# Expert 0's gate and up products ahead of the last two groups of the gather, in PSUM bank 6

## What is computed

```python
g_p, g_idx = lax.top_k(jax.nn.softmax(g_logits, axis=-1), 1)      # one of 4 groups
e_top, e_idx = lax.top_k(e_logits, TOP_K_IN_GROUP)                # 2 of its 8 experts
gate = g_p * jax.nn.softmax(e_top, axis=-1)
...
def expert_block(args):
    xb, e = args
    return (jax.nn.silu(xb @ w_gate[e]) * (xb @ w_up[e])) @ w_down[e]
...
x = x + hier_moe(h2, ...)
return rmsnorm_2(x, norm_f_g)
```

## Time and profile before

| | |
|---|---|
| runs of the kernel | 764.04, 763.16, 762.18 us; median 763.16 |
| profiled execution | span 760.7 us from the first to the last instruction (its time on the device is not listed apart; the median lies 2.5 us above the span) |
| TensorE busy | 727.5 us, 96% of the span |
| VectorE, ScalarE, GpSimd busy | 364.0, 324.0, 80.4 us |
| read from HBM | 179.91 MB |
| granted clock of TensorE, mean | 0.986 of 2.4 GHz |

### The profile page before, as it was taken

The page is one execution under the profiler, slowest core; times in us unless marked ns, Lnnn a source line. Parts: engine busy times, 40 slices in busy tenths (PEclk is TensorE's granted clock), DMA queues, the critical chain, the costliest instruction groups (busy, mean ns, idle before and its releaser), DMA issues.

```text
span 760.7 us, 11630 instructions
## 1 busy us (share of the span) xinstructions
PE 727.5 (96%) x4414; PEld 528.2 (69%) x4414; DVE 364.0 (48%) x602; ACT 324.0 (43%) x534; POOL 80.4 (11%) x58
## 2 busy tenths in 40 slices
PE   7999999899999999989999999988999999999994
PEld 6887864789999999959979999866333333333332
DVE  3244433656655655865544646655233323333224
ACT  3143444355445445554626443333334333343333
POOL 0000000132344332310030000000000000000001
PEclk9999999999999999999999999978999999999998
DMA  8951313245545545533423455482999999999992
GB/s 354 424 194 56 111 55 117 104 168 174 208 172 180 206 165 185 202 111 111 167 111 120 158 191 197 166 337 88 393 423 422 424 423 423 423 422 423 424 420 90
DMA packets 25237, 181.48 MB, mean 239 GB/s; under 512 B 2800, under 2 KB 3056, under 8 KB 3568
## 3 DMA queue, kind: packets, MB, share of 16 engines
q1 hardware_dynamic: 25056, 180.90, 60.7%
q10 hardware_dynamic: 144, 0.07, 0.0%
HBM read 179.91 MB, written 1.05 MB: 238 GB/s over the span
## 4 chain that ended last, share of the span: by engine, by line
PE 84%; DVE 6%; DMA 4%; ACT 2%; issue 1%; POOL 1%; SPq 0%; POOLq 0%; DVEq 0%; ACTq 0%
PE psum L861 39%; PE psum L1079 13%; PE psum L1092 6%; PE psum L1101 5%; PE psum L557 4%; PE psum L655 4%; DMA HN<-units_in 3%; PE psum L565 3%; PE psum L614 2%; DVE ffn_w_low L448 2%; PE psum L1071 1%; POOL rstd L1638 1%; DVE arena L1909 1%; PE psum L1050 1%; ACT ffn_w_high L443 1%
## 5 line engine op out<-in xcount | busy, mean ns | idle before, releaser
L448 DVE TENSOR_TENSOR ffn_w_low<-ring,ffn_w_high 128x2048 fp32r<-128x2048 f32 x57 | 134.7, 2364 | 119.5 <-ACT ffn_w_high L443 119.4
L443 ACT ACTIVATE ffn_w_high<-ring 128x2048 fp32r<-128x2048 f32 x57 | 109.3, 1918 | 144.9 <-PE psum L861 144.6
L861 PE MATMUL psum<-ht_high,ffn_w_high 128*128 128x256 f32 x576 | 163.8, 284 | 2.3 <-DVE ht_low L1893 1.3
L861 PE MATMUL psum<-ht_low,ffn_w_high 128*128 128x256 f32 x576 | 163.0, 283 | 0.0
L861 PE MATMUL psum<-ht_high,ffn_w_low 128*128 128x256 f32 x576 | 163.0, 283 | 0.0
L861 PEld LDWEIGHTS psum<-ht_high,ffn_w_high 128*128 128x128 f32 x576 | 110.4, 192 | 4.1 <-issue 2.1
L861 PEld LDWEIGHTS psum<-ht_low,ffn_w_high 128*128 128x128 f32 x576 | 110.5, 192 | 0.3
L861 PEld LDWEIGHTS psum<-ht_high,ffn_w_low 128*128 128x128 f32 x576 | 110.5, 192 | 0.0
L1254 ACT ACTIVATE arena<-psum 64x512 f32<-64x512 f32 (+6 forms) x96 | 43.0, 453 | 128.8 <-PE psum L1079 102.3
L2223 DVE TENSOR_TENSOR arena<-psum,arena 64x512 f32<-64x512 f32 x32 | 21.9, 684 | 126.4 <-ACT arena L1254 126.4
L1638 POOL TENSOR_TENSOR rstd<-ms,neghalf 128x1 f32<-128x1 f32 (+3 forms) x19 | 15.2, 803 | 509.1 <-DVE ms L1692 369.8
(11 more groups left out here) (308 smaller groups left out, 1104.0 us busy)
## 6 DMA issues: line engine op xcount, KB each, us to landing
ring<-units_in SPq DMA_DIRECT2D x117, 1024.0 KB, 5.0
more_units<-units_in SPq DMA_DIRECT2D x32, 1024.0 KB, 17.1
HN<-units_in SPq DMA_DIRECT2D x8, 1024.0 KB, 18.2
rows<-units_in SPq DMA_DIRECT2D x8, 1024.0 KB, 17.3
rows<-rows_in SPq DMA_DIRECT2D x1, 1688.0 KB, 12.6
arena<-bias_in SPq DMA_DIRECT2D x1, 1536.0 KB, 15.9
small<-small_in SPq DMA_DIRECT2D x1, 1232.0 KB, 25.4
const<-const_in SPq DMA_DIRECT2D x1, 1073.0 KB, 23.2
```

What stands on the lines that cost most here:

```text
L443: nc.scalar.activation(parts_slot(n)[0], w, ACT.Copy).then_inc(hi_ready, 1)
L448: nc.vector.tensor_tensor(l, ring[:, n % RING, :], h.bitcast(fp32), SUB).then_inc(lo_ready, 1)
L861: last = mm(o, l[a], r[b], start=start and (a, b) == pairs[0], stop=stop and (a, b) == pairs[-1])
```

## The change

The products of expert 0 move from behind the whole gather to behind its group 5, that is between groups 5 and 6 (the second half of the slots is groups 4 to 7). They are written into bank 6 instead of bank 0, and ScalarE and VectorE read them there. TensorE waits for `xw_ready` 1 at the new place; the wait for `xs_act` 4 falls away. SyncE's program and the order of the instructions on ScalarE and VectorE are as they were.

```diff
+        FIRST_AFTER, FIRST_BANK = 5, 6
...
+            def expert_up(x, w, ks, bank=0):
+
+                for k in ks:
+                    a, r = k % HALF_K * 2 * D_EXP, CH * (k % 2)
+                    last = mm(psum[r:r + CH, bank, :], x[:, k, :], w[:, a:a + 2 * D_EXP], start=k < 2, stop=k >= KD - 2)
+                return last
...
                 last.then_inc(xs_done, 1)
-
-            def expert_up(x, w, ks):
-
-                for k in ks:
-                    a, r = k % HALF_K * 2 * D_EXP, CH * (k % 2)
-                    last = mm(psum[r:r + CH, 0, :], x[:, k, :], w[:, a:a + 2 * D_EXP], start=k < 2, stop=k >= KD - 2)
-                return last
+                if g == FIRST_AFTER:
+                    pe.wait_ge(xw_ready, 1)
+                    for h in range(2):
+                        expert_up(XW[:, 0], unit(pe, U_EXP + h), range(h * HALF_K, (h + 1) * HALF_K), FIRST_BANK
+                                  ).then_inc(unit_used, 1)
...
-            pe.wait_ge(xs_act, 4)
-            pe.wait_ge(xw_ready, 1)
-            for g in range(2):
-                expert_up(XW[:, 0], unit(pe, U_EXP + g), range(g * HALF_K, (g + 1) * HALF_K)).then_inc(unit_used, 1)
             pe.wait_ge(table_in, 1)
...
-                copy(TS[0:CH, :], psum[CH:P, 0, :]).then_inc(low_half, 1)
+                copy(TS[0:CH, :], psum[CH:P, FIRST_BANK if e == 0 else 0, :]).then_inc(low_half, 1)
...
-                tt_op(UG[0:CH, :], psum[0:CH, 0, :], TS[0:CH, :], ADD).then_inc(up_summed, 1)
+                tt_op(UG[0:CH, :], psum[0:CH, FIRST_BANK if e == 0 else 0, :], TS[0:CH, :], ADD).then_inc(up_summed, 1)
```

## The result

| | median, us | runs | ratio to before, 95% interval |
|---|---|---|---|
| before | 762.75 | 5 | |
| after | 766.71 | 5 (765.22 to 768.23) | 1.0054 (1.0034 to 1.0073) |
| after, measured again beside the experiments | 766.28 | 8 (763.61 to 768.26) | 1.0058 (1.0037 to 1.0080) |

The change makes the kernel slower by 0.54 to 0.58%, 4.1 to 4.4 us; 2.3 us were forecast. The interval does not hold 1.0, so the loss is clear of the noise, small as it is. The plain difference of the medians is 3.96 us in both comparisons. The profiled execution of after has a span of 764.9 us against 760.7, and its own time is 766.71.

What follows compares the result with a forecast made beforehand. The prediction took the weight stream to set the end, with TensorE having slack. Its terms, +3.6 - 1.3 + 0 = +2.3 us on a median of 763.16, gave 765.5 us, range 763.7 to 767.2.

Steps and rivals of the forecast that it cites:

- The bound: End of the expert stage: the weight stream sets the end, and TensorE has 2.5 us of slack.
- Term 1: SyncE's issue into rows: released later because the gather's group 7 ends later, +3.6 us on the stream's start.
- Term 2: First 9 us of the weight stream: three queued units remove the 361 GB/s dip, -1.3 us, bounds 0 and -2.1.
- Term 3: TensorE from expert 1 on: 2.6 us later, covered by slack at the end, so 0 us.
- The cover: End of the kernel: TensorE's 2.5 us slack plus the stream's 2.3 us delay, 4.8 us, absorbs TensorE's 2.6 us lateness.
- Rival B: TensorE around expert 1: the clock falls after a thin stretch; 767.5 us if for 8 us of dense work; chance 0.07.
- Rival A: Start of the weight stream: nothing is caught up, 361 GB/s for its first 9 us; +3.6 us, 766.8 us; chance 0.15.
- Rival C: First 2.83 us of the weight stream: queued units fill the engines faster, catch-up -2.1 us, 764.7 us; chance 0.15.
- Rival D: TensorE sets the end and expert 0's sums overlap groups 6 and 7; -0.5 us, 762.7 us; chance 0.06.

Runs made afterwards that it cites:

- e1: The changed kernel with expert 0's products put back behind the whole gather, still in bank 6; 762.18 us, ratio 0.9994 to before.
- e5: The changed kernel with expert 0's copies, sums and SiLU ahead of the last gather takes, expert 1's window start loaded early; 764.89 us, ratio 1.0033 to before.
- e11: The changed kernel again, not edited, profiled once more; 765.94 us, a single run.
- e10: The changed kernel again, not edited, for one look at its profile; 766.09 us, a single run.
- e2: The kernel before with only SyncE's issue into rows held back until expert 0's second half unit is used; 764.54 us, ratio 1.0018 to before.
- e4: The changed kernel with useless matmuls in TensorE's idle time, one before the table and two behind it; 764.68 us, ratio 1.0024 to before.
- e7: The changed kernel again, not edited, beside other experiments; 766.28 us, eight runs.
- e12: The kernel before again, not edited, for one look at its profile; 759.09 us, a single run.
- e6: The changed kernel with the edits of e3 and e5 together; 762.87 us, ratio 1.0010 to before.
- e8: e6 with one useless matmul added between the gather and the table; 762.58 us, ratio 1.0008 to before.
- e3: The changed kernel with SyncE issuing the two units freed by expert 0's products ahead of the one into rows; 764.95 us, ratio 1.0036 to before.

## Why the prediction was right in its sign and too small

**The bound.** Right: the stream of weights sets the end in all profiles, and e1 shows that the place makes the loss.

**Term 1, +3.6 us on the stream's start.** Right in kind, a little small. With an ordinary gather the issue into rows stands 13.1 to 13.3 us behind the gather's start (e5, e11, e10) against 9.3: +3.8 to 4.0. Of this 3.58 are the products; groups 6 and 7 take 2.10 us behind them in place of 1.87. In the profile shown first, another 0.9 was the late rise of the clock in the gather, which is chance.

**Term 2, -1.3 us of catch-up.** This is the step that failed. The mechanism was right as long as TensorE is in time: e2, e4 and e5 have the full rate at once, and their streams are 1.1 to 2.2 us shorter than those of before. In the changed kernel next to nothing was caught up (213.1 to 213.9 against 213.2 to 214.2), because the fourth and fifth unit came late: 6.9 and 9.9 us behind the issue into rows, where e4 has them 6.1 and 8.3 us behind it, and the full rate. The prediction's test was too weak as well: it asked only that the fourth come before the work queued is done. The fourth did, at 540.70, 3.2 us before the third landed (543.9), and still the fourth, fifth and sixth landed 2.8, 3.2 and 3.6 us apart in place of 2.5. Why the DMA slows down while units are still under way is not shown.

**Term 3, 0 us for TensorE's lateness.** Its size without the clock was right: 2.6 us forecast for expert 1's start, and 537.76 - 534.25 = 3.5 measured, of which 0.9 is the later end of the gather. The cover was judged wrongly. The 4.8 us of slack at the end do cover TensorE's own work. But a late TensorE also releases slots late, and in its first 20 us the stream has none to spare. The prediction checked this only for the fourth unit and only with the fast clock.

**Rival B, the clock, at 0.07.** It took place in all four profiles. The mean clock of a run cannot tell whether it also did in the others: after has 0.982, and so have e4 and e5, without the fall. The clock fell after 4.03 us with 1.08 busy, and not after the stretch from 136.25 to 140.89, 4.64 us with 2.16 busy. Its price was sought at the end of the kernel, where the slack covers it, and not at the release of units. With e4 beside the changed kernel the fall costs 1.1 to 1.9 us of stream (212.0 against 213.1 to 213.9), and by the ratios, 1.0024 against 1.0054 and 1.0058, 2.3 to 2.6 us, of which the late rise in the gather may be a part. The Trainium skill ("TensorE: Matmul & The Clock Gate", section "Part 1: The HAM clock gate") says that the slow clock is the default and that sustained activity releases it. That spoke for B. The trace agrees: after the thin stretch the clock was 1.2 GHz for some 3.4 us in four of four profiles.

**Rival A, +3.6 us,** came nearer in number, and next to nothing was caught up, as it said. Its reason does not hold: three units queued at once do not slow the stream (e2 begins with three and has 422 GB/s). The catch-up was lost because the fourth and fifth unit came late. That this costs about what A had for another reason, and so puts 766.71 beside A's 766.8, is luck. The Trainium skill's limit of about 358 GB/s per core ("DMA: Bandwidth & Descriptors", section "Where 436 GB/s comes from") did not hold here: behind the first 20 us the trace of every kernel has 422 or 423 GB/s for some 190 us. **Rival C** fell with the same 174 to 185 GB/s in the first 2.83 us of e5, after, e7, e10 and e11. **Rival D** fell with the waits for DMA at the end.

**The sum with measured terms:** +3.9 for the start, -0.1 for the catch-up (the means 213.55 of four profiles of after and 213.69 of before, e12 and e1), 0 at the end: +3.8, against 4.1 and 4.4 measured, whose intervals begin at 2.6 and 2.8 us. The late rise of the clock in the gather, 0.9 us in two of the four profiles of after, is not in this sum.

What stays open: what makes the stream slow in its first 20 us while issued units are still under way. It is clearest in e6 and e8, whose stream starts as early as in before and which still show 381 to 382 GB/s in their second 9 us. Only e3 shows the plain case of no unit left. No experiment was made on the rest.

## What to carry to other kernels

When a kernel ends on a stream of transfers, look for what releases its first one, and ask of each moved step which release stands behind it. Slack at the end protects only an engine's own work: if the engine also frees buffers, its lateness can be charged where the buffers are scarce, here at the start of the stream. And a new wait on TensorE should be priced together with the clock behind it; e4 and e5 show two ways out, work to fill it or a shorter wait. None of the versions here beat the kernel before.

## What the runs showed of the hardware

- TensorE did some 1.08 us of narrow matmuls in 4.01 to 4.03 us (after, e7, e10, e11), and its clock then fell to 1.2 GHz for some 3.4 us. It fell 0.1 to 1.3 us after dense work had begun again. After 1.08 us in 2.08 (e5), and after 3.69 us in 4.01 (e4), it stayed at 2.4.
- The same stretch of the same kernel meets the clock in different states: 64 matmuls of the gather took 9.26 us (before) and 7.74 us (e12). The runs of this kernel range from 759.1 to 764.9 us, with medians of 762.3 to 763.2.
- Loads of 1024 KB from HBM kept 423 GB/s for 201 us on one core (before, 541 to 742), and 421 to 423 for over 200 us in e2, e4 and e5, where the stream has no dip.
- From issue to landing a load of 1024 KB took 4.7 to 4.9 us with no other under way (before 4.7, e2 4.8, e5 4.9), and 9 to 12 us with three or four others under way (before 9.2 to 10.8, e2 9.2 to 12.3).
